# Neighbouring rows of the experts' matrices in one partition, and the gather reordered to match

## The reference

```python
def hier_moe(x, w_group, b_group, w_expert, b_expert, w_gate, w_up, w_down):
    ...                      # picks a group, then 2 of its 8 experts for each token: expert, gate
    y = grouped_experts(xf, expert, gate, w_gate, w_up, w_down)

def expert_block(args):      # in grouped_experts, for the rows of tokens that chose expert e
    xb, e = args
    h = jax.nn.silu(xb @ w_gate[e]) * (xb @ w_up[e])
    return h @ w_down[e]
# y = sum over a token's two experts of gate * row
```

## Time and profile before

| what | value |
|---|---|
| median of 3 runs | 3524.98 us (3524.2 to 3525.24) |
| profiled execution | 3526.45 us, its span 3524.3 us |
| TensorE busy | 3212.5 us, 91% of the span |
| weight loads busy | 1896.8 us, 54% (beside the matmuls) |
| VectorE, ScalarE, GpSimd busy | 751.2, 492.1, 99.1 us |
| moved by DMA | 702.74 MB, mean 199 GB/s |
| loads of in_moe_w_gate, in_moe_w_up, in_moe_w_down | 128 DMAs of 1024 KB each |
| mean granted TensorE clock | 0.951 of full speed |

### The profile page before, as it was taken

The page is one execution under the profiler, slowest core; times in us unless marked ns, Lnnn a source line. Parts: engine busy times, 40 slices in busy tenths (PEclk is TensorE's granted clock), DMA queues, the critical chain, the costliest instruction groups (busy, mean ns, idle before and its releaser), DMA issues.

```text
span 3524.3 us, 33898 instructions
## 1 busy us (share of the span) xinstructions
PE 3212.5 (91%) x13674; PEld 1896.8 (54%) x13674; DVE 751.2 (21%) x1680; ACT 492.1 (14%) x885; POOL 99.1 (3%) x48
## 2 busy tenths in 40 slices
PE   9699997999999996999978898999997898999997
PEld 4357744677457743577547664444433565444443
DVE  1430013100130014300434403111112413111112
ACT  0220002000120002100111111111111301111111
POOL 0000000000000000000000100000000000000000
PEclk9799997999999997999967998999998998999999
DMA  7334441444434432244312243999997243999996
GB/s 255 99 109 154 155 153 47 155 157 152 144 111 152 155 128 91 96 144 153 120 32 106 72 160 112 395 393 394 395 395 261 96 148 108 340 395 393 394 395 262
DMA packets 359176, 702.74 MB, mean 199 GB/s; under 512 B 20524, under 2 KB 113194, under 8 KB 359076
## 3 DMA queue, kind: packets, MB, share of 16 engines
q1 hardware_dynamic: 357808, 699.46, 55.9%
q10 hardware_dynamic: 1268, 1.83, 0.2%
HBM read 698.36 MB, written 1.05 MB: 198 GB/s over the span
## 4 chain that ended last, share of the span: by engine, by line
issue 98%; POOL 2%; POOLq 0%; DVE 0%; DVEq 0%
POOL roots L1702 2%; POOLq L166 0%; DVE x L1769 0%; POOLq L1701 0%; POOLq L1702 0%; POOL roots L1696 0%; POOL roots L1697 0%; DVEq L1768 0%; POOLq L2433 0%
## 5 line engine op out<-in xcount | busy, mean ns | idle before, releaser
L610 PE MATMUL lin<-ring,arena 128*128 128x512 f32 (+4 forms) x3600 | 1325.9, 587 | 44.4 <-DVE arena L2271 16.7
L610 PEld LDWEIGHTS lin<-ring,arena 128*128 128x128 f32 (+1 forms) x3600 | 552.1, 176 | 727.6 <-issue 704.4
L610 PE MATMUL sco<-arena,ring 128*128 128x256 f32 (+1 forms) x2836 | 620.2, 380 | 9.6 <-DVE arena L2220 9.0
L610 PEld LDWEIGHTS sco<-arena,ring 128*128 128x128 f32 x2836 | 540.6, 191 | 98.4 <-issue 16.7
L610 PE MATMUL sco<-ring,arena 128*64 128x512 f32 (+2 forms) x2132 | 465.1, 583 | 30.7 <-DMA ring<-in_moe_w_up 27.6
L610 PEld LDWEIGHTS sco<-ring,arena 128*64 128x64 f32 (+1 forms) x2132 | 164.3, 142 | 329.2 <-issue 322.8
L610 PE MATMUL lin<-arena 128*128 128x128 f32 (+8 forms) x1592 | 293.4, 376 | 23.4 <-DVE arena L2084 11.8
L610 PEld LDWEIGHTS lin<-arena 128*128 128x128 f32 (+3 forms) x1592 | 181.7, 189 | 130.1 <-issue 93.5
L1905 DVE TENSOR_TENSOR arena<-arena,sco 128x256 f32<-128x256 f32 x88 | 37.1, 421 | 821.2 <-ACT arena L1472 821.2
L1702 POOL TENSOR_TENSOR roots<-roots 128x8 f32<-128x8 f32 x42 | 98.7, 2351 | 3418.9 <-DVE roots L1748 3418.9
L2281 DVE TENSOR_TENSOR arena<-arena,sco 128x512 f32<-128x512 f32 x32 | 22.0, 688 | 720.2 <-PE sco L610 720.2
(11 more groups left out here) (230 smaller groups left out, 1296.8 us busy)
## 6 DMA issues: line engine op xcount, KB each, us to landing
ring<-in_moe_w_gate SPq DMA_DIRECT2D x128, 1024.0 KB, 14.9
ring<-in_moe_w_up SPq DMA_DIRECT2D x128, 1024.0 KB, 14.2
ring<-in_moe_w_down SPq DMA_DIRECT2D x128, 1024.0 KB, 14.2
ring<-in_w_gate_up SPq DMA_DIRECT2D x88, 1024.0 KB, 5.1
ring<-in_w_down SPq DMA_DIRECT2D x44, 1024.0 KB, 4.9
ring<-in_w_in_a SPq DMA_DIRECT2D x24, 1024.0 KB, 6.9
ring<-in_w_out SPq DMA_DIRECT2D x16, 1024.0 KB, 5.1
ring<-in_xa_wkv SPq DMA_DIRECT2D x16, 1024.0 KB, 5.2
```

The source lines that it names most:

```text
L610: return nc.tensor.matmul(o, lhsT, rhs, start=start, stop=stop)
```

## The change

The matrices of the experts are loaded with the neighbouring rows 4p to 4p + 3 (gate, up) or 2p and 2p + 1 (down) of a part in partition p. Block k of a slot then holds the features 4p + k of its half, or 2p + k of its half, and the other factor of each product must come in the same order. So `gather` takes every fourth column of x, beginning with k, as its stationary operand, and the transposes of `pair_h` take every second column. The products are sums over the same terms in another order. The path for overflow keeps the order it had. The instructions are otherwise the same, in number and in order.

```diff
-                def pieces(e):
+                def pieces(e, order):
 
                     for name in ("moe_w_gate_2", "moe_w_up_2"):
                         for k in range(2):
-                            yield A[name][layer, e, k * 512:(k + 1) * 512, :].rearrange("(k p) n -> p k n", p=P)
+                            yield A[name][layer, e, k * 512:(k + 1) * 512, :].rearrange(order, p=P)
                     for f in range(2):
-                        yield A["moe_w_down_2"][layer, e, f * 256:(f + 1) * 256, :].rearrange("(k p) n -> p k n", p=P)
+                        yield A["moe_w_down_2"][layer, e, f * 256:(f + 1) * 256, :].rearrange(order, p=P)
 
                 with rounds(sp, PAIRS, {free: RING}) as i:
-                    first, second = list(pieces(i * 2)), list(pieces(i * 2 + 1))
+                    first, second = [list(pieces(i * 2 + n, "(p k) n -> p k n")) for n in range(2)]
...
-                        for n, src in enumerate(pieces(i)):
+                        for n, src in enumerate(pieces(i, "(k p) n -> p k n")):
...
                     for half in range(2):
-                        for j in range(4):
-                            b = 4 * half + j
+                        every_fourth = x[:, :, half * 512:(half + 1) * 512].rearrange("p t (f k) -> p t k f", k=4)
+                        for k in range(4):
                             for t in range(NT):
-                                last = mm(trp[:, banks[half], j * P:(j + 1) * P], x[:, t, b * P:(b + 1) * P], gathering[:, t, :],
+                                last = mm(trp[:, banks[half], k * P:(k + 1) * P], every_fourth[:, t, k, :], gathering[:, t, :],
                                           start=t == 0, stop=t == NT - 1)
...
-                    for f in range(4):
-                        last = nc.tensor.transpose(trp[:, banks[0], f * P:(f + 1) * P], pair_h[:, f * P:(f + 1) * P], ident[:, :])
+                    for half in range(2):
+                        every_second = pair_h[:, half * 256:(half + 1) * 256].rearrange("p (f k) -> p k f", k=2)
+                        for f in range(2):
+                            b = 2 * half + f
+                            last = nc.tensor.transpose(trp[:, banks[0], b * P:(b + 1) * P], every_second[:, f, :], ident[:, :])
```

## The result

The changed kernel takes 3624.19 us (median of 4 runs, 3623.93 to 3625.12) against 3525.11 us (3524.2 to 3526.15, 4 runs) for the one before: ratio 1.0281, 95% interval 1.0264 to 1.0299. It is 99 us slower, where 31 us faster was forecast, and outside the range given.

A forecast was written before the change was run, and what follows sets the result against it. Late pairs of both expert layers were taken as DMA-bound, with TensorE's 29.97 us a pair as floor. Loads -15.5 - 15.5, gather 0, transposes 0: -31.0 us from 3524.98 to 3494.0 us, range 3486 to 3575.

The forecast's parts named there:

- Two regimes: In each expert layer, early pairs run at TensorE's 29.97 us, late pairs at DMA's 31.91 us with waits for loads.
- the store of twelve slots: Load slots filled before each expert loop feed seven pairs at TensorE's pace and cover a DMA shortfall of 13.6 us.
- the DMA period from the size of the pieces: Expert loads: 2 KB rows at 387 GB/s and 4 KB rows at 410 give 31.91 us a pair.
- The loads: Expert loads in 8 KB pieces: 423 GB/s, 29.8 us a pair, saving 15.5 us in each of two layers.
- the lower bound: Expert loads cut at 4 KB: 410 GB/s, 30.69 us a pair, shortfall 10.8 us, still covered by the store.
- The transposes: Four transposes of pair_h reading every second float32: taken as 0, bounded by 14 us if doubled.
- The gather: Gather's weight loads reading x 16 bytes apart on TensorE's chain: taken as no added cost over 1088 loads.
- the "doubled" rival: Strided read doubles the gather's loads to 208 ns: +101 us, 3595 us in all; chance 0.17.
- break-even: Gather: 28 ns more per instruction, a load of 143 instead of 104 ns, would use up the 31.0 us saved.
- the bounds I gave: Gather's strided loads: from nothing to 416 ns a load, +327 us.
- weak nearest row: Gather's existing side-by-side load, 128 columns of the same tensor; said to support the zero-cost choice only weakly.
- faster, within and slower: Chances for the whole kernel's time against no change, told apart at about 0.2%, 7 us: 0.66, 0.10, 0.28.

The follow-up runs named there:

- TensorE lightened: New 8 KB loads and operands read side by side, with half the gather's instructions left out: 3459.41 us beside 3530.45 us for the kernel before.

## Why the prediction was wrong

**What bounds the kernel: right.** Two regimes, the store of twelve slots and the DMA period from the size of the pieces were all borne out. With TensorE lightened, the same two regimes come back, with a store of some 13 us.

**The loads: right in mechanism and size.** -31.0 us was forecast for them; the two runs that keep the old gather show 0.9906, the one with x copied 0.9907, -33 us by the ratio, with the interval from -25 to -41 us; by the medians the three are 30.3, 31.0 and 33.5 us under the kernel before. 8 KB pieces run at 422 GB/s (423 forecast), 4 KB pieces at 410, and the lower bound suffices, as argued.

**The transposes: right in size.** Taken at nothing, they cost 0.03 us for four, with no difference in time between the runs with and without the stride. That their load would grow from 141 to 201 ns was not foreseen; it hides.

**The gather: this step failed.** I took its strided load at nothing. It costs 3.90 us a gather, 132.6 us in all, over the "doubled" rival's 101 us. I had seen the price of failure (break-even at 28 ns an instruction) and that load and matmul were balanced; both stand. The sign named for this failure, a period above 30 us from the first pair on, is what the trace shows. The wrong inference was this one: the transposes draw 128 columns in 141 ns, so the read path can deliver columns twice as fast, so a halved delivery would fit. It counted columns, and it carried a transpose's load over to a matmul's, which the runs show to behave otherwise. They say that the gather's operand is paid by the 16-byte unit. From the time between two starts in a gather:

| distance | 16-byte units for 128 columns | measured between starts | for a unit |
|---|---|---|---|
| 4 bytes | 32 | 0.115 us | bound by the matmul |
| 8 bytes | 64 | (4.04 - 0.28) / 31 = 0.121 us | 1.9 ns |
| 12 bytes | 96 | (5.84 - 0.34) / 31 = 0.177 us | 1.85 ns |
| 16 bytes | 128 | (7.74 - 0.40) / 31 = 0.237 us | 1.85 ns |
| 32 bytes | 128 | (7.88 - 0.41) / 31 = 0.241 us | 1.88 ns |

The number subtracted in each row is the length of one MATMUL. The first row is the matmul's own pace: before, eight matmuls of 512 columns take 3.70 us, 0.116 us for each 128 columns. The row at 8 bytes lies so near it that it says little of the price; the other three carry it.

The row that I used gives nearly this price when it is divided by bytes. With 85 ns of latency (137 less 64 columns at 0.81 ns), the 141 ns for 128 contiguous float32 are 56 ns for 32 units, 1.75 ns a unit; 128 units then take 224 ns, 109 ns over the interval of 0.115 us, and 1088 x 109 ns = +119 us. That is inside the bounds I gave, and the forecast would have been 3613 us. Seen from behind this is in part luck: the row is a transpose's, and the loads of the transposes don't follow that price when their operand is strided.

The Trainium skill, SBUF — State Buffer, section "Specifications (TRN2)", asks for two hits on each 16-byte line; the gather agrees with it, 0.121 us at two columns a line and 0.237 at one; the transposes, 0.63 us for four at two and at one, do not show it. I gave the doubled read 0.17 against a weak nearest row. The case of three columns in four taking a fresh line, 0.177 us, lies between, so in the gather it is a price for each line more than a threshold.

**A sum that doesn't close.** The chances of faster, within and slower, 0.66, 0.10 and 0.28, add up to 1.04; by the parts given, slower should be 0.24.

**What followed.** Since the gather sits on the chain that sets TensorE's period, its 3.9 us raised the period above DMA's 31.91 us, and with that the gain of the loads went too. The gain was not offset, it was removed: the gather alone costs as much as the whole change.

**Open.** The load of a transpose takes 141 ns side by side but 196 to 203 ns at 8, 12 and 16 bytes, alike. The unit price would give some 320 ns at 16. Since the four transposes themselves take only 0.63 us, the record alone can't be at fault; why a transpose escapes the price no run here tells. So the price per unit is shown for float32 matmuls of this shape, not for every read of TensorE, and the cause can lie in the matmul's way of reading, or in the tensor read (the matmuls read only x at a stride, the transposes only pair_h). Nor was it tried whether an operand of another type would pay the same.

## What to carry to other kernels

When a layout is changed for the sake of DMA, price the other end of it: here 8 KB pieces raised the rate that the loads can reach from 395 to 422 GB/s, and the matching stride of 16 bytes doubled the time of a product on the critical chain. Price the strided operand of such a matmul by the 16-byte units it touches (1.85 ns each here), and measure that price on the instruction you are going to change: a row of another kind of instruction misled this forecast. If an operand is read many times, put it in order once where an engine waits anyway (2 us a layer here), or stop at two neighbouring rows, which kept two float32 in each unit and some three quarters of the gain (0.9926 against 0.9906 and 0.9907, with intervals that overlap).

## What the runs showed of the hardware

The rate of 1 MiB loads by contiguous piece: 387 GB/s at 2 KB, 410 at 4 KB, 422 at 8 KB, to which a fixed 9.6 ns a piece and 75.1 ns for each 2 KB on one of 16 engines fit. The moving operand of the gather pays nearly as the stationary one does (0.229 us against 0.237 for 128 columns at 16 bytes). Transposes are all but indifferent (0.63 us for four at 8 and at 16 bytes, 0.60 side by side). VectorE's copy with a strided read at 16 bytes takes 2.06 us for two tiles of 128x1024; a copy of such a tile that reads runs of 64 side by side takes 0.69 us (line 2144 of the kernel before).
